# A time mixer with five runs of small products a period in place of seven, and new orders on TensorE, ScalarE and VectorE

## What is computed

```python
def rwkv7_scan(r, w, k, v, kk, a):
    def step(S, inp):
        r_t, w_t, k_t, v_t, kk_t, a_t = inp
        sa = jnp.einsum('bhij,bhj->bhi', S, -kk_t)
        S = (S * w_t[:, :, None, :]
             + sa[..., None] * (kk_t * a_t)[:, :, None, :]
             + v_t[..., None] * k_t[:, :, None, :])
        y_t = jnp.einsum('bhij,bhj->bhi', S, r_t)
        return S, y_t
...
    decay = jnp.exp(-DECAY_SCALE * jax.nn.sigmoid(w0 + jnp.tanh(wl) @ w_w2))
    a = jax.nn.sigmoid(a0 + al @ w_a2)
    g = jax.nn.sigmoid(gl) @ w_g2
    kk = heads(k * k_k)
    kk = kk / jnp.maximum(jnp.linalg.norm(kk, axis=-1, keepdims=True), 1e-12)
    k = k * (1.0 + (a - 1.0) * k_a)
...
    y = rwkv7_scan(r_h, w_h, k_h, v_h, kk, a_h)
    ym = jnp.mean(y, axis=-1, keepdims=True)
    yv = jnp.mean(jnp.square(y - ym), axis=-1, keepdims=True)
    y = ((y - ym) * lax.rsqrt(yv + GN_EPS)).reshape(B, T, RWKV_DIM) * gn_g + gn_b
    bonus = jnp.sum(r_h * k_h * r_k, axis=-1, keepdims=True) * v_h
    y = (y + bonus.reshape(B, T, RWKV_DIM)) * g
```

## Time and profile before

| | |
|---|---|
| time, 3 runs | 2405.33 us median (2404.95 to 2405.37) |
| profiled execution | span 2404.5 us, 0.8 us under the median; the page gives no time of its own beside the span |
| TensorE busy | 2157.6 us (90%), VectorE 1529.0 (64%), ScalarE 684.3 (28%), GpSimd 659.7 (27%) |
| front stage, 0 to 53.3 us | TensorE busy 48.47 us |
| mixer stage, 53.3 to about 681 us | TensorE busy 623.33 us, VectorE 506.20, ScalarE 316.04; clock 1.00, DMA share 0.37 |
| merge, about 681 to 1098 us | TensorE busy 415.37 us, DMA share 0.69 |
| experts, 1098 us to the end | TensorE busy 1070.47 us, DMA share 1.00 |

### The profile page before, as it was taken

The page is one execution under the profiler, slowest core; times in us unless marked ns, Lnnn a source line. Parts: engine busy times, 40 slices in busy tenths (PEclk is TensorE's granted clock), DMA queues, the critical chain, the costliest instruction groups (busy, mean ns, idle before and its releaser), DMA issues.

```text
span 2404.5 us, 37848 instructions
## 1 busy us (share of the span) xinstructions
PE 2157.6 (90%) x15331; PEld 1510.5 (63%) x15331; DVE 1529.0 (64%) x2605; ACT 684.3 (28%) x1366; POOL 659.7 (27%) x539
## 2 busy tenths in 40 slices
PE   9999999999999999998999889978877787777776
PEld 8999999999899999987554444433332233222222
DVE  7778888888765455548876567667446444444445
ACT  6555555455344444432121111111011000000000
POOL 1000000000000000004554555555455445444442
PEclk9999999999999999999999999999999999999999
DMA  6533333333367666679999999999999999999997
GB/s 213 141 95 98 102 88 101 103 88 98 106 184 194 185 187 187 190 270 342 417 427 424 425 423 426 427 427 426 427 427 428 426 427 427 427 427 427 427 427 289
DMA packets 348320, 708.19 MB, mean 295 GB/s; under 512 B 13834, under 2 KB 272482, under 8 KB 281826
## 3 DMA queue, kind: packets, MB, share of 16 engines
q0 software_dynamic: 74176, 537.01, 53.1%
q1 hardware_dynamic: 273732, 168.55, 24.1%
q10 hardware_dynamic: 240, 0.22, 0.0%
HBM read 703.63 MB, written 2.10 MB: 294 GB/s over the span
## 4 chain that ended last, share of the span: by engine, by line
DMA 36%; PE 17%; issue 2%; DVE 2%; POOL 1%; DVEq 0%; ACT 0%; POOLq 0%; ACTq 0%
DMA query_w<-in_v_table,experts 17%; DMA rows<-in_v_table,experts 13%; PE bank L1980 7%; PE project L1980 4%; DMA rows<-in_u_table,experts 3%; DMA up_rows<-in_u_table,experts 3%; PE bank L247 2%; DMA down_row_more<-in_v_table,experts 2%; PE bank L1896 2%; PE project L247 1%; PE bank L1938 0%; PE bank L1944 0%; PE bank L1612 0%; PE bank L1923 0%; POOL rows L1851 0%
## 5 line engine op out<-in xcount | busy, mean ns | idle before, releaser
L2102 DVE CUSTOM_DVE_ANT_0 rows<-rows,h 128x2048 f32<-128x2048 f32 x170 | 388.7, 2292 | 329.7 <-DMA rows<-in_u_table,experts 329.5
L1851 POOL DMA_INDIRECT rows<-in_u_table,experts x170 | 182.9, 1076 | 1097.7 <-DVE experts L1449 1040.0
L232 DVE TENSOR_TENSOR w_half_rest<-w_half,w_half_high 128x1024 fp32r<-128x1024 f32 x224 | 271.4, 1219 | 160.5 <-ACT w_half_high L211 160.3
L247 PE MATMUL project<-hT_high,w_half_high 128*128 128x272 f32 (+1 forms) x1152 | 351.1, 305 | 0.4 <-PEq L254 0.3
L1980 PE MATMUL bank<-query_w,merged_spare 128*128 128x512 f32 x608 | 283.6, 602 | 60.7 <-DMA query_w<-in_v_table,experts 47.3
L1980 PE MATMUL bank<-rows,merged_spare 128*128 128x512 f32 x612 | 286.4, 605 | 57.2 <-DMA rows<-in_v_table,experts 43.8
L247 PE MATMUL project<-hT,w_half_high 128*128 128x272 f32 (+1 forms) x1152 | 329.2, 286 | 0.0
L247 PE MATMUL project<-hT_high,w_half_rest 128*128 128x272 f32 (+1 forms) x1152 | 328.7, 285 | 0.0
L2102 DVE CUSTOM_DVE_ANT_0 up_rows<-up_rows,h 128x2048 f32<-128x2048 f32 x86 | 197.0, 2292 | 168.7 <-DMA up_rows<-in_u_table,experts 168.7
L211 ACT CAST w_half_high<-w_half 128x1024 fp32r<-128x1024 f32 x224 | 234.9, 1051 | 204.3 <-PE merge_ps L247 120.6
L1980 PEld LDWEIGHTS bank<-rows,merged_spare 128*128 128x128 f32 x612 | 114.0, 192 | 223.2 <-issue 127.3
(11 more groups left out here) (435 smaller groups left out, 3760.3 us busy)
## 6 DMA issues: line engine op xcount, KB each, us to landing
w_half<-in_w_in SPq DMA_DIRECT2D x176, 512.0 KB, 4.1
w_half<-in_w_branch_a SPq DMA_DIRECT2D x32, 512.0 KB, 3.9
out_w<-in_w_out SPq DMA_DIRECT2D x16, 1024.0 KB, 5.6
w_half<-in_w_branch_b SPq DMA_DIRECT2D x16, 512.0 KB, 3.9
query_w<-in_w_q_peer SPq DMA_DIRECT2D x8, 1024.0 KB, 16.2
out_w<-in_w_q_peer SPq DMA_DIRECT2D x6, 1024.0 KB, 19.1
lora_weights<-in_w_in SPq DMA_DIRECT2D x4, 896.0 KB, 14.1
rows<-in_u_table,experts POOLq DMA_INDIRECT x170, 21.1
```

Source lines behind the costliest of these rows:

```text
L232: return eng.tensor_tensor(low.bitcast(F32R), x, high, ALU.subtract)
L247: mm = nc.tensor.matmul(out, a.bitcast(F32R), b.bitcast(F32R), start=start and n == 0, stop=stop and n == 2)
L1851: pool.indirect_dma_start(ur[n % RU], None, w["u_table"][0], bass.IndirectOffsetOnAxis(ap=k.idx[:, t, h, j:j + 1], axis=0)).then_inc(s_u[n ...
L2102: v.tensor_tensor_reduce(ur[n % RU], ur[n % RU], k.h[:, n // (HEADS * TOPK), :], 1.0, 0.0, ALU.mult, ALU.add, dots(n, n + 1)).then_inc(s_d ...
```

## The change

The three order tables are new. On TensorE the 48 slices of a period stand in five stretches (10, 6, 10, 11, 11) in place of seven (10, 3, 3, 6, 8, 8, 10). `gv` moves to stage 4 and right in front of `lw`; `gr` is cut into two units; `rb` moves to the end of the period; `Z` 5, `gr` 0, `s` 4 and `T` 5 stand in one run. ScalarE takes two steps over from VectorE: the scaling of the decay sigmoid (`lw`, semaphore `sg`) and `k_scale` (new unit `lt`, semaphore `rate`). The copies `cv` and of the norm vectors go: the vectors are read in place (`k.vec`). Cut to its core:

```diff
 PE_ORDER = (
-    ("t", 1, 2), ("rb", 0, 2), ("u", 0, 3), ("lw", 0, 1), ("f", 10, 0), ("s", 0, 3), ("Z", 1, 2), ("r", 1, 3), ("la", 0, 1),
...
+    ("t", 1, 2), ("u", 0, 3), ("Z", 1, 2), ("gv", 0, 4), ("lw", 0, 1), ("f", 10, 0),
+    ("s", 0, 3), ("T", 1, 2), ("r", 1, 3), ("la", 0, 1), ("f", 6, 0),
+    ("u", 1, 3), ("T", 2, 2), ("s", 1, 3), ("r", 2, 3), ("lg", 0, 1), ("f", 10, 0),
...
+    ("u", 4, 3), ("Z", 5, 2), ("gr", 0, 1), ("s", 4, 3), ("T", 5, 2), ("t", 0, 1), ("gr", 1, 1), ("r", 0, 2), ("rb", 0, 1),
 )
...
-            def gr(_, p, par):
+            def gr(i, p, par):
 
                 wait(pe, q["st"], p + 1)
-                wait(pe, q["kst"], p + 1)
-                wait(pe, q["Zst"], p * 5)
-                wait(pe, q["off"], p)
-                for n, lhs in ((0, bst), (2, kst)):
-                    for c in range(NCH):
-                        mm = by_head(inv[n][:, c * CH:(c + 1) * CH], lhs[:, c, :], ast[par][:, c, :])
-                    mm.then_inc(q["gram"], 1)
+                if i:
+                    wait(pe, q["kst"], p + 1)
+                    wait(pe, q["Zst"], p * 5)
+                else:
+                    wait(pe, q["off"], p)
+                for c in range(NCH):
+                    mm = by_head(inv[2 * i][:, c * CH:(c + 1) * CH], (bst, kst)[i][:, c, :], ast[par][:, c, :])
+                mm.then_inc(q["gram"], 1)
...
             def gv(_, p, par):
                 wait(pe, q["sqr"], p + 1)
+                if p + 1 < PAIRS:
+                    wait(pe, q["Uc"], p * 5 + 6)
...
                 nc.scalar.activation(sg[:, real], low[:, 0:T], ACT.Tanh, scale=0.5, bias=k.vec[:, V_W0H, p:p + 1]).then_inc(q["sig"], 1)
+                wait(act, q["sig"], p * 3 + 1)
+                nc.scalar.activation(sg[:, real], sg[:, real], ACT.Copy, scale=0.5, bias=0.5).then_inc(q["sg"], 1)
...
+            def lt(_, p, par):
+                wait(act, q["rk"], p)
+                wait(act, q["sig"], p * 3 + 2)
+                nc.scalar.activation(t1[:, real], am[:, real], ACT.Identity, scale=k.vec[:, V_KAH, p:p + 1],
+                                     bias=k.vec[:, V_KAC, p:p + 1]).then_inc(q["rate"], 1)
...
-            def cv(_, p, par):
-                d()
-                n.tensor_copy(cur[par][:], k.vec[:, :, p]).then_inc(q["rm"], 1)
...
             def la(_, p, par):
-                wait(dve, q["sig"], p * 3 + 1)
-                n.tensor_scalar(sg[:, real], sg[:, real], 0.5, 0.5, ALU.mult, ALU.add)
-                d()
+                wait(dve, q["sg"], p + 1)
                 n.tensor_tensor_scan(cs[:, real], k.const[:, C_SCAN + PAD:C_SCAN + TP], sg[:, real], 0.0, ALU.mult, ALU.add)
-                wait(dve, q["sig"], p * 3 + 2)
-                n.tensor_scalar(t1[:, real], am[:, real], cur[par][:, V_KAH:V_KAH + 1], cur[par][:, V_KAC:V_KAC + 1], ALU.mult, ALU.add)
                 d()
                 n.tensor_tensor(csm[:, real], cs[:, real], sg[:, real], ALU.subtract).then_inc(q["csum"], 1)
...
             def ge(_, p, par):
-                n.tensor_copy(gcur[:], k.vec[:, V_GNG:V_GNB + 1, p])
```

More of the change, by code:

```diff
@@ L653, in rwkv_stage @@
         ww2, wa2, wg2 = sb("w_decay2", [DECAY_LORA, P]), sb("w_rate2", [ICL_LORA, P]), sb("w_gate2", [P, 2, P])
-        cur, gcur, eps = two("pair_vectors", [P, NVEC]), sb("pair_norm_vectors", [P, 2]), sb("group_norm_eps", [P, 1])
+        eps = sb("group_norm_eps", [P, 1])
         r, kx, v = two("r", [P, TP]), two("k", [P, TP]), two("v", [P, TP])
@@ L679, in rwkv_stage @@
         c3 = lambda t, n=CH: t.rearrange("p (c t) -> p c t", t=n)
-        names = ("lora_w", "own", "shifted", "rm", "lora_mm", "sig", "csum", "exps",
+        names = ("lora_w", "own", "shifted", "lora_mm", "sig", "csum", "exps",
                  "ksq", "norm", "nroot", "rk", "bonus", "bonr", "st", "kst", "vst", "endc", "gram",
@@ L684, in rwkv_stage @@
                  "rhs", "rhsc", "U", "Uc", "Snew", "S", "Yo", "Yc", "sqr", "var", "vsqrt",
-                 "done", "zero", "rst", "y", "yhigh")
+                 "done", "zero", "rst", "y", "yhigh", "sg", "rate")
         q = {n: k.sem(f"r_{n}") for n in names}
@@ L910, in e @@
                 if i == 0:
-                    wait(act, q["rm"], p + 1)
                     wait(act, q["st"], p - 1)
@@ L914, in e @@
                 wait(act, k.s_used, p * 6 + 2 * i + 2)
-                nc.scalar.activation(t[:, real], pr[(3 * p + i) % 2][:, 0:T], ACT.Copy, scale=cur[par][:, o:o + 1]).then_inc(q["own"], 1)
+                nc.scalar.activation(t[:, real], pr[(3 * p + i) % 2][:, 0:T], ACT.Copy, scale=k.vec[:, o, p:p + 1]).then_inc(q["own"], 1)
             def kn_(_, p, par):
@@ L919, in kn_ @@
                 wait(act, q["st"], p)
-                nc.scalar.activation(kn[:, real], kx[par][:, real], ACT.Copy, scale=cur[par][:, V_KK:V_KK + 1])
+                nc.scalar.activation(kn[:, real], kx[par][:, real], ACT.Copy, scale=k.vec[:, V_KK, p:p + 1])
             def sq_(_, p, par):
@@ L924, in sq_ @@
                 wait(act, q["norm"], p)
-                nc.scalar.activation(sq[:, real], kx[par][:, real], ACT.Square, scale=cur[par][:, V_KK:V_KK + 1]).then_inc(q["ksq"], 1)
+                nc.scalar.activation(sq[:, real], kx[par][:, real], ACT.Square, scale=k.vec[:, V_KK, p:p + 1]).then_inc(q["ksq"], 1)
             def lw(_, p, par):
@@ L934, in la @@
                 wait(act, q["lora_mm"], p * 3 + 2)
-                nc.scalar.activation(am[:, real], low[:, 0:T], ACT.Tanh, scale=0.5, bias=cur[par][:, V_A0H:V_A0H + 1]).then_inc(q["sig"], 1)
+                nc.scalar.activation(am[:, real], low[:, 0:T], ACT.Tanh, scale=0.5, bias=k.vec[:, V_A0H, p:p + 1]).then_inc(q["sig"], 1)
             def lg(_, p, par):
@@ L1003, in _ @@
             wait(act, q["zero"], n_zero)
-            schedule(ACT_ORDER, {"split": sp_, "e": e, "kn": kn_, "sq": sq_, "lw": lw, "la": la, "lg": lg, "ex": ex, "nm": nm, "ab": ab, "t": t,
+            schedule(ACT_ORDER, {"split": sp_, "e": e, "kn": kn_, "sq": sq_, "lw": lw, "la": la, "lt": lt, "lg": lg, "ex": ex, "nm": nm, "ab": ab, "t": t,
                                  "r": r_, "u": u_, "yc": y, "gv": gv, "ge": ge, "lo": lo, "yf": yf})
@@ L1051, in lk @@
             def lk(_, p, par):
-                d()
+                wait(dve, q["rate"], p + 1)
                 n.tensor_tensor(k2[:, real], kx[par][:, real], t1[:, real], ALU.mult)
                 d()
-                n.scalar_tensor_tensor(out=rk[:, CH:TP], in0=r[par][:, CH:TP], scalar=cur[par][:, V_RK:V_RK + 1], in1=k2[:, CH:TP],
+                n.scalar_tensor_tensor(out=rk[:, CH:TP], in0=r[par][:, CH:TP], scalar=k.vec[:, V_RK, p:p + 1], in1=k2[:, CH:TP],
                                        op0=ALU.mult, op1=ALU.mult).then_inc(q["rk"], 1)
@@ L1178, in go @@
                 d()
[L1179 removed]
+                n.scalar_tensor_tensor(out=yc[:], in0=yc[:], scalar=k.vec[:, V_GNG, p:p + 1], in1=rstd[:], op0=ALU.mult, op1=ALU.mult)
                 d()
[L1181 removed]
+                n.scalar_tensor_tensor(out=yc[:], in0=yc[:], scalar=k.vec[:, V_GNB, p:p + 1], in1=bon[p % 3][:], op0=ALU.add, op1=ALU.add)
                 d()
@@ L1192, in _ @@
             wait(dve, q["zero"], n_zero)
-            schedule(DVE_ORDER, {"split": rest, "cv": cv, "e": e, "la": la, "lk": lk, "nr": nr, "bo": bo, "ks": ks, "rs": rs, "kb": kb,
+            schedule(DVE_ORDER, {"split": rest, "e": e, "la": la, "lk": lk, "nr": nr, "bo": bo, "ks": ks, "rs": rs, "kb": kb,
                                  "gr": gr, "gm": gm, "rb": rb, "Z": Z, "T": T_, "r": r_, "s": s_, "ge": ge, "go": go, "gy": gy})
```

7 lines of the change are left out of this document (3 added, 4 removed), and 27 rows, old and new, of tables (ACT_ORDER, DVE_ORDER, PE_ORDER).

## The result

The changed kernel takes 2470.9 us (median of 4 runs, 2469.25 to 2472.61) against 2405.35 us for the kernel before: a ratio of 1.0271 [1.0256, 1.0286] (in brackets, here and below, the interval that holds the ratio with 95%). It is slower by 65.5 us. The profiled execution has a span of 2469.0 us, against 2404.5. The forecast was 2460 us, in a range of 2438 to 2477.

What follows compares the result with a forecast made beforehand. The prediction took TensorE, busy 35.00 of 35 us in the mixer, as the bound. Its terms, -11 + 37 + 16 + 1 + 4 + 8 = +55 us on 2405.33, gave 2460 us, range 2438 to 2477.

Steps and rivals of the forecast that it cites:

- The first wait: TensorE at T 5 waits for VectorE's last-level mask behind R_st: 2.65 us in 14 periods, +37 us.
- The second wait: TensorE at r 2 waits for the state after chunk 1: 1.3 us a period, +16 us over 13 periods.
- The borders: Fewer changes between projection and small products on TensorE: -0.56 us a period, -11 us for 18 periods.
- VectorE's relief is worth nothing: Work taken off VectorE, about 1.0 us a period, gains nothing, as its idle time is in front of R_st.
- The clock: TensorE's clock falls to half behind five of 14 gaps, at most 1.7 us each: +8 us, bounds 0 to +24.
- the second rival: TensorE's clock falls at nearly every gap, 14 x 1.7 = 24 in place of 8: 2476 us; chance 0.18.
- The period of 38.5 to 39 us, given as a sign: In the mixer's profile after, the square of y comes every 38.5 to 39 us, not 35.30.
- The end of the stage: Last weight splits behind the group norm and a pooling window, TensorE having only slices left: +4 us, bounds -1 and +7.
- The first: First rival: only the T 5 wait shows, the chunk 1 state wait stays 0.3 us, clock up: 2440 us; chance 0.15.
- the third rival: Faster: the last level's mask is in time for T 5, only the borders count: 2394 us; chance 0.05.

Runs made afterwards that it cites:

- e1: Changed kernel with the last level's mask (Z 5) moved ahead of R_st in VectorE's order: 2422.45 us, ratio 1.0062.
- e6: Changed kernel with ScalarE's copy of U of chunk 1 put ahead of the take-over of projection tile 0: 2473.3 us, ratio 1.0275.
- e10: Changed kernel with mask ahead of R_st, weight split 3 behind the state after chunk 1, and copy of U first: 2407.99 us, ratio 1.0003.
- e11: As e10, with the stage's last three weight splits at their ordinary places in the order: 2404.55 us, ratio 0.9987.
- e8: Kernel before, with one run of small products cut in three by two projection slices: 2416.56 us, ratio 1.004.
- e3: Changed kernel with the two scalings (decay sigmoid and k_scale) back on VectorE: 2487.42 us, ratio 1.0331.
- e5: Changed kernel with only VectorE's weight split 3 moved behind the state after chunk 1: 2471.54 us, ratio 1.0263.
- e2: Changed kernel with six unread products of 272 columns filling TensorE's gap before T 5: 2463.65 us, ratio 1.023.
- e9: Changed kernel with the edits of e5 and e2 together (split late, gap filled): 2452.99 us, ratio 1.0193.

## Why the prediction was right, and where it was off

**The first wait: right, to 0.01 us.** Forecast 2.65 us in 14 periods, 37; measured 2.64 in 14, 37. e1 takes it away and shows that the falls of the clock go with it.

**The second wait: right.** Forecast 1.3 us a period, 1.2 more than before, 16 in all; measured 1.28. The chain from state to state was 6.37 us for a forecast of 6.3. The row of the waits alone shows only 11.0 for it, because part of the time stands in the same run in front of `U`; e6 shows that these two are one cost.

**The borders: right in kind, a little too large.** Forecast -0.56 us a period. With it the period without a fall comes out: 35.30 + 2.64 + 1.28 - 0.56 = 38.66, measured 38.66; that it does to the last digit is partly luck, for e10 and e11 show the term by itself: with both waits away the new order has 34.84 us a period, 0.46 under the earlier trace rows. e8, which adds borders to the old order, prices one at 0.335, more than the 0.29 of the forecast; what takes the rest in the new order stays open. Over the whole stage less still is left of it: from the first to the last square of y e10 takes 519.9 us, the kernel before 522.3, since some of its periods are 35.1 to 35.7 us long.

**"VectorE's relief is worth nothing": wrong.** The step looked only for idle time in front of `R_st`. The two scalings would also stand in the chain between the two states, and there they are worth 0.7 us a period (e3). The sum was not hurt, since the chain had been added up from the instructions of the new order, without them.

**The clock: mechanism right, size too small.** Forecast five falls of 1.7 us, +8; measured nine of 1.55, +14, midway between the forecast and the 14 falls of the second rival. The bounds, 0 to 24, held it. The count came from two gaps in another stage, and that was too thin. The period of 38.5 to 39 us, given as a sign, came only where no fall stood in it; elsewhere it was 40.2. Falls behind nearly every gap, as in the second rival, come in e3 (14 of 14) and e5 (13 of 14). The Trainium skill, TensorE: Matmul & The Clock Gate, Why this matters for your kernels, asks for no idle gap between bursts of matmuls above a bound, since such a gap puts the engine back to half clock; the bound that it gives is longer than the 2.48 us here. By it none of the 14 gaps would bring a fall. Nine do, and the measurement decides; that it is the idle gap that brings them, e2 shows, at 0 falls against nine.

**The end of the stage: too small.** Forecast +4, bounds -1 and +7. The four terms above (37, 17, 14 and -10 for 18 borders) are 58 of the 66.6 us by which the last projection product is late. The 8.6 that remain lie in the wait of 3.58 us with half clock behind it, in a wait of 2.0 us for the state at 712 us with another stretch of half clock, and at the start of the stage; I have not separated them. The largest part is behind the last output: from the last square of y to the last projection product it is 12.3 us, where the kernel before has 10.3 and does ten slices more in them. e11 against e10 prices the wait of 3.58 us at 3.4, net of the 2.1 that come back in front of the merge. Behind the stage 2 us come back: until TensorE's work ends, the expert stage has two clock falls where the kernel before has seven. No run tests that.

The forecast of 2460 us was 11 us low: 6 by the falls and some 5 by the end of the stage; 2 came back in the expert stage, and the other 2 I put down to rounding and the way from the profiled execution to the median; no run separates them. So the 11 us are two terms that were too small, less a gain that nobody had forecast. The first and the third rival fell: the second wait shows in full, and `T` 5 starts 2.64 us late in 14 periods.

## What to carry to other kernels

Where an order table puts a consumer right behind a producer, read the other engine's queue: the mask was ready to be made, and stood behind an instruction that waits for exactly that producer. Price the clock with the gap: a gap of 2.5 us on TensorE cost another 1.55 us in nine cases of 14, and a saving elsewhere in the period can be eaten by more such falls, so take away the gap first. Fewer runs of small products were worth 0.23 us each here (0.46 for two, e10), and only when both engines' orders kept their waits covered.

## What the hardware showed that I had not expected

- The same gap of 2.48 us brings a fall to half clock or brings none: nine of 14 in the changed kernel, 13 in e5, all 14 in e3. Length alone doesn't decide it; in e3 one also came behind a wait of 1.47 us. What does is not settled; the three kernels differ in when the gap comes and in what TensorE does in between.
- In the changed kernel the clock falls 0.2 to 1.4 us after TensorE has started again; in e5 it is down with the first product after the gap in nine of 14, and stays down for 6.8 us in four.
- A wait of 1 us removed from a period of 40 us gave nothing (e5), and 0.84 us a period once the gap was filled (e9).
- Unread products in place of idle time made the kernel faster by 0.4% (e2, 1.023 against 1.0271), although they were 0.42 us too long.
